# One body of an attention loop turned by one weight unit: each pass projects the next pass's queries among its own scores

## The reference

```python
def mixer_inputs(h, pos, p):
    q_r, k_r, v_r, g_r, q_d, k_d, v_d, ga, gb = jnp.split(h @ p['w_in'], points, axis=-1)
    q_d = rope(rmsnorm(q_d.reshape(B, L, N_DIFF_HEADS, 2, DIFF_HD), p['q_norm_g']), pos, DIFF_ROT, ROPE_THETA)
    k_d = rope(rmsnorm(k_d.reshape(B, L, N_DIFF_HEADS, 2, DIFF_HD), p['k_norm_g']), pos, DIFF_ROT, ROPE_THETA)
...
def layer_prompt(x, pos, p, lam_init):
    h = rmsnorm(x, p['norm1_g'])
    (q_r, k_r, v_r, g_r), (q_d, k_d, v_d), (ga, gb) = mixer_inputs(h, pos, p)
    o_r, S = retention_prompt(q_r, k_r, v_r)          # 4 heads, 128 wide keys, 256 wide values
    ...                                                # differential attention: 8 heads, two softmaxes each
    x = x + mixer_output(o_r, g_r, o_d, ga, gb, p, lam_init)
    f, conv_state = conv_glu(rmsnorm(x, p['norm2_g']), zeros, p)
    return x + f, (k_d, v_d, S, conv_state)
```

## Time and profile before

| | us |
|---|---|
| median of 3 runs | 2384.08 |
| the three runs | 2384.08, 2383.68, 2388.91 |
| profiled execution, whole | 2388.49 |
| its span, first to last instruction | 2386.6 |
| PE busy | 2297.6 |
| VectorE busy | 1131.4 |
| ACT busy | 966.5 |
| POOL busy | 851.3 |

### The profile page before, as it was taken

How to read it: one execution, slowest core, us unless ns; L and a number is a source line. 1 busy time by engine, 2 the same in 40 slices (tenths; PEclk the granted TensorE clock), 3 DMA queues, 4 the chain that set the end, 5 groups by cost and what they waited for, 6 DMA issues and landing times.

```text
span 2386.6 us, 50229 instructions
## 1 busy us (share of the span) xinstructions
PE 2297.6 (96%) x17560; PEld 2188.9 (92%) x17560; DVE 1131.4 (47%) x1918; ACT 966.5 (40%) x1829; POOL 851.3 (36%) x380
## 2 busy tenths in 40 slices
PE   5999999999999999999999999999999999999999
PEld 5788889889999999999988898798999999999999
DVE  3644453333545576156344644533345455742663
ACT  3544553333423343244335545533343234422443
POOL 3243232223433343343451342232333443434433
PEclk9999999999999999999999999999999999999999
DMA  4132212121222222322232122122122222223223
GB/s 150 51 102 70 85 60 68 60 90 60 89 72 89 83 88 70 108 89 73 80 99 72 63 83 85 51 83 86 60 72 75 72 89 89 84 75 101 90 67 105
DMA packets 81237, 193.28 MB, mean 81 GB/s; under 512 B 7232, under 2 KB 36000, under 8 KB 81056
## 3 DMA queue, kind: packets, MB, share of 16 engines
q1 hardware_dynamic: 59120, 172.38, 22.0%
q10 hardware_dynamic: 21936, 18.56, 2.4%
HBM read 177.50 MB, written 13.42 MB: 80 GB/s over the span
## 4 chain that ended last, share of the span: by engine, by line
issue 57%; PE 25%; POOL 14%; DVE 2%; ACT 1%; POOLq 0%; DVEq 0%; ACTq 0%
POOL wlo L490 11%; PE ps L602 6%; PE ps L604 6%; PE ps L603 6%; POOL rstd L496 3%; PE ps L961 2%; PE ps L962 2%; PE ps L963 2%; DVE ca L1943 1%; PE ps L641 0%; PE ps L642 0%; PE ps L643 0%; PE ps L669 0%; DVE af L1957 0%; DVE odif L1828 0%
## 5 line engine op out<-in xcount | busy, mean ns | idle before, releaser
L490 POOL TENSOR_TENSOR wlo<-raw,whi 128x1024 fp32r<-128x1024 f32 (+1 forms) x330 | 758.7, 2320 | 1338.4 <-ACT whi L1007 1338.4
L602 PE MATMUL ps<-hl,whi 128*128 128x272 f32 x2496 | 723.6, 290 | 2.4 <-DVE hl L1847 2.4
L604 PE MATMUL ps<-hl,wlo 128*128 128x272 f32 x2496 | 719.6, 288 | 0.0
L603 PE MATMUL ps<-hl,whi 128*128 128x272 f32 x2496 | 718.2, 288 | 0.0
L602 PEld LDWEIGHTS ps<-hl,whi 128*128 128x128 f32 x2496 | 471.6, 189 | 4.3 <-issue 2.8
L604 PEld LDWEIGHTS ps<-hl,wlo 128*128 128x128 f32 x2496 | 470.1, 188 | 0.0
L603 PEld LDWEIGHTS ps<-hl,whi 128*128 128x128 f32 x2496 | 469.7, 188 | 0.0
L641 PE MATMUL ps<-whi,hl 128*128 128x256 f32 x1536 | 446.6, 291 | 11.7 <-ACT rk L1234 10.2
L642 PE MATMUL ps<-wlo,hl 128*128 128x256 f32 x1536 | 438.9, 286 | 0.0
L643 PE MATMUL ps<-whi,hl 128*128 128x256 f32 x1536 | 438.1, 285 | 0.0
L1007 ACT ACTIVATE whi<-raw 128x1024 fp32r<-128x1024 f32 (+1 forms) x330 | 313.2, 996 | 224.0 <-PE ps L963 177.2
(11 more groups left out here) (214 smaller groups left out, 2926.5 us busy)
## 6 DMA issues: line engine op xcount, KB each, us to landing
raw<-in_w_units_dram SPq DMA_DIRECT2D x266, 512.0 KB, 4.7
raw<-in_w_down_units_dram SPq DMA_DIRECT2D x64, 352.0 KB, 3.3
out_new_k_prompt_dram<-rawk ACTq DMA_DIRECT2D x8, 512.0 KB, 3.0
out_new_v_prompt_dram<-vd ACTq DMA_DIRECT2D x8, 512.0 KB, 3.0
x<-in_x_dram ACTq DMA_DIRECT2D x8, 272.0 KB, 11.4
out_y_dram<-x SPq DMA_DIRECT2D x8, 272.0 KB, 5.7
kc_n<-in_cache_k_dram SPq DMA_DIRECT2D x8, 256.0 KB, 2.9
vc_n<-in_cache_v_dram SPq DMA_DIRECT2D x8, 256.0 KB, 3.3
```

The lines of the kernel that those rows point to most:

```text
L490: ins = e.tensor_tensor(wlo[:, s, a:b], raw[:, s, a:b], whi[:, s, a:b].bitcast(F32), ALU.subtract)
L602: e.matmul(out, wh, hi, start=(c == 0), stop=False)
L603: e.matmul(out, wh, lo, start=False, stop=False)
L604: ins = e.matmul(out, wl, hi, start=False, stop=(c == KC - 1))
```

## The change

- Phase S now has a unit, the queries of the first pass of D. They are computed chunk by chunk for four tiles at once, in the banks t, o, s0, s1 and s0b, and the statistics follow them. The last chunk's squares are added on VectorE, so PE's statistics need 6 matmuls in place of 12.
- A pass of D begins with the keys (unit 0), then values (1), gate (2), and the next pass's queries (3); in the last pass unit 3 is the queries and keys of retention head 0. Gate and queries are 72 chunks in one list, `FILL`: 16 ahead of the scores, five at each of the ten steps, the rest at the end.
- R is one body over four heads, without its first unit. The scaling of `oret` of a head is spread over the tiles of the next head's first unit.

```diff
-ORDER = [("S", 1), ("D", 4), ("R", 2), ("M", 1), ("F", 1), ("G", 1)]
+ORDER = [("S", 1), ("D", 4), ("R", 1), ("M", 1), ("F", 1), ("G", 1)]
...
+        UNITS = dict(S=1, D=4, R=11, M=16, F=FB + KC, G=FB + KC)
...
         def slot(phase, j):
-            return (j + (phase == "G")) % 2
+            return (j + (phase in ("D", "R", "G"))) % 2
...                                              PE, phase S
-                    stats("s0")
+                    e.wait_ge(*S.at("w_ready", k=0))
+                    for m in range(TILES):
+                        acquire(S_BANKS[m], act=1, dve=int(m == NT))
+                    for c in range(KC):
+                        for m in range(NT):
+                            if m in (0, 2):
+                                half_ready(c, m // 2)
...
+                    stats("s1b")
...                                              PE, phase D
-                    n_unit(0, hl1, xs, before=lambda m: e.wait_ge(*S.at("xs_ready", k=0)) if m == NT else None, chunk=half_ready)
+                    n_unit(0, hl1, xs)
...
-                    n_unit(1, hl1, xs)
-
...
-                    n_unit(2, hl1, xs, after=queries)
+                    n_unit(1, hl1, xs, after=queries)
                     cached_keys(0)
-                    e.wait_ge(*S.at("w_ready", k=3))
-                    t_tile(3, 0, 0, hl1, act=1)
+
+                    filled = [0, None]
...
+                    fill(FILL_FIRST)
...
-                        gate_chunks(GATE_SHARE[n])
+                        fill(FILL_SHARE[n])
...
+                    fill(len(FILL) - filled[0])
                     values(9)
...
-        GATE_SHARE = (3, 2, 2, 2, 1, 2, 2, 2, 4, 4)
+        FILL = ([("g", t, c) for t in range(4) for c in range(KC)] + [("q", t, c) for t in range(NT) for c in range(KC)]
+                + [("s", 0, c) for c in range(KC)])
+        FILL_FIRST = 16
+        FILL_SHARE = (5, 5, 5, 5, 5, 5, 5, 5, 5, 5)
...                                              ACT, phase D
+                    square(rawq, "q")
                     prev = None
                     t = 0
-                    for u, (name, buf) in enumerate((("q", rawq), ("k", rawk), ("v", vd))):
+                    for u, (name, buf) in enumerate((("k", rawk), ("v", vd))):
...
+                    hi("D", 3, 0)
+                    hi("D", 3, 1)
                     e.wait_ge(*S.at("t_ready", ("kc", 0)))
...
+                                if tt == 3:
+                                    hi("D", 4, 0)
+                                    hi("D", 4, 1)
...                                              ACT, phase R
+                                if u == 0 and m:
+                                    scale_ret(hh - 1, m - 1)
...
-                        e.wait_ge(*S.at("dve_step", ("rsr", hh)))
-                        for m in range(TILES):
...                                              VectorE, phase D
-                    sample_sum(rawq[0:DEC, NT, :], "mm0", ("N", 0, 4), "q")
                     qk_sums("q")
-                    qk_apply(rawq, "q", 0, lambda: sample_sum(rawk[0:DEC, NT, :], "mm1", ("N", 1, 4), "k"))
+                    qk_apply(rawq, "q", 0)
+                    sample_sum(rawk[0:DEC, NT, :], "mm0", ("N", 0, 4), "k")
                     qk_sums("k")
...
-                    sample_sum(vd[0:DEC, NT, :], "mm0", ("N", 2, 4), "v")
+                    sample_sum(vd[0:DEC, NT, :], "mm1", ("N", 1, 4), "v")
```

More of the change, by code:

```diff
@@ L375, in units @@
                     for c in range(KC)]
[L376 to L379 removed]
+            return [wide(FIRST[phase] + q) for q in range(UNITS[phase])]
         def prep_len(phase, j):
@@ L614, in stats @@
                 for m, a, b in blocks:
-                    for n, t in enumerate((acc[:, a:b], sq[:, 1, a:b])):
-                        ins = e.matmul(pv(bank, b - a, 1, m), t, one[:, :], start=(n == 0), stop=(n == 1))
+                    ins = e.matmul(pv(bank, b - a, 1, m), acc[:, a:b], one[:, :], start=True, stop=True)
                 ins.then_inc(*S.up("st_ready", "stats"))
@@ L775, in values @@
                         ins.then_inc(*S.up("o_ready", (hh, ib)))
[L777 to L795, removed]
                     scores(0)
@@ L986, in program, with filled_at @@
         SOFF = [0, 512, 896, 1152]
-        GATE_SHARE = (3, 2, 2, 2, 1, 2, 2, 2, 4, 4)
-        GATE_AT = [next(n for n in range(10) if sum(GATE_SHARE[:n + 1]) >= KC * t) for t in (1, 2, 3)]
+        FILL = ([("g", t, c) for t in range(4) for c in range(KC)] + [("q", t, c) for t in range(NT) for c in range(KC)]
+                + [("s", 0, c) for c in range(KC)])
+        FILL_FIRST = 16
+        FILL_SHARE = (5, 5, 5, 5, 5, 5, 5, 5, 5, 5)
+        FILL_DONE = {}
+        for end in range(KC, len(FILL) + 1, KC):
+            kind, t, _ = FILL[end - 1]
+            FILL_DONE[(kind, t)] = ([-1] if end <= FILL_FIRST else []) + [
+                n for n in range(10) if FILL_FIRST + sum(FILL_SHARE[:n + 1]) >= end] + [10]
+        def filled_at(n):
+            return [tile for tile, at in FILL_DONE.items() if at[0] == n]
         def act_program(S):
@@ L1549, in dve_program, with sample_sum @@
             with S.layers() as l:
+                def sample_sum(buf, bank, key, *name):
+                    e.wait_ge(*S.at(f"act_free_{bank}", ("rest",) + key))
+                    e.wait_ge(*S.own())
+                    e.scalar_tensor_tensor(out=buf, in0=pv(bank, DEC, UC), scalar=rs1[0:DEC, NT:TILES], in1=rest[:, 0:UC],
+                                           op0=ALU.mult, op1=ALU.add).then_inc(*S.up(f"dve_free_{bank}", ("rest",) + name))
                 with S.body("S"):
-                    norm_mean("s0")
+                    norm_mean("s1b")
                     e.wait_ge(*S.at("rs_ready", "rstd"))
                     e.tensor_scalar(hr[:, :], rs1[:, :], 0.5, None, ALU.mult).then_inc(*S.up("dve_step"))
+                    e.wait_ge(*S.at("pool_step", "zeroed"))
+                    sample_sum(rawq[0:DEC, NT, :], S_BANKS[NT], ("N", 0, NT), "q")
                 with S.body("D") as p:
@@ L1556, in dve_program @@
                     e.wait_ge(*S.at("pool_step", k=0))
-                    def sample_sum(buf, bank, key, name):
-                        e.wait_ge(*S.at(f"act_free_{bank}", ("rest",) + key))
-                        e.wait_ge(*S.own())
-                        e.scalar_tensor_tensor(out=buf, in0=pv(bank, DEC, UC), scalar=rs1[0:DEC, NT:TILES], in1=rest[:, 0:UC],
-                                               op0=ALU.mult, op1=ALU.add).then_inc(
-                            *S.up(f"dve_free_{bank}", ("rest", name)))
                     def qk_sums(name):
```

346 lines of the change are left out of this document (209 added, 137 removed).

## The result

| | us |
|---|---|
| changed kernel, median of 4 runs | 2577.91 (2574.07 to 2580.09) |
| kernel before, median of 4 runs | 2385.27 (2383.68 to 2388.91) |
| ratio, 95% interval | 1.0804 (1.0787 to 1.082) |
| profiled execution, whole and span | 2580.09, 2578.3 |

What follows compares the result with a forecast made beforehand. PE's own work plus its little waiting was taken to bound the kernel. 2386.6 + 189 (D) + 34 (clock) - 2 (layer starts) - 13 (R) = 2595 us of span; forecast time 2591 us, range of 8 in 10 2550 to 2635.

Steps and rivals of the forecast that it cites:

- The two chains: In D, the queries' and keys' paths over ACT, POOL and VectorE: two new PE waits, 27.0 us a pass together.
- the tiles and with the releasers named: PE waits at the values' second tile for the keys' sample sum, at the second gate tile for the values'.
- the steps of 13.8 and 13.2 us per pass: PE's predicted stands in each D pass: 13.8 us from the queries' chain, 13.2 us from the keys'.
- the sum: Forecast span of the whole program, all terms added to the earlier 2386.6 us: 2595 us.
- The scores: In D's softmax steps, thicker filling covers 1.2 of PE's 1.7 us idle a pass, bounds 0 and 1.7.
- The clock: Slow pace after D's stalls: 2.6 us for each of 16, +42 us; earlier falls go, -8; net +34.
- The starts of the layers: PE's statistics finish sooner, -3.6 and -5.5 us, but a wait for ACT gives back 3.4 each: -2.3 together.
- R: Retention phase: PE's 10.2 us of waits for ACT go, with their gaps and one clock fall: -12.7 us.
- the last rival: D's stalls as forecast, but the clock costs only 1.5 us for each: 2573 us; chance 12%.
- The one for the faster side: In D, the queries' rope is done ahead of use if their power isn't held behind `lo` 2: 2334 us; 5%.

Runs made afterwards that it cites:

- pow_q: Changed kernel with only the queries' power moved on POOL, from behind `lo` 2 to behind `lo` 1: 2520.58 us.
- pow_both: Changed kernel with both powers moved on POOL, the queries' ahead of `lo` 2 and the keys' ahead of `lo` 3: 2405.61 us.
- sums_first: Changed kernel with VectorE's sample sums of keys and values put ahead of the scaling and rope of queries and keys, POOL's order untouched: 2533.43 us.
- kept_busy_all: Changed kernel with 109 and 105 matmuls of unused result added on PE ahead of the two waits of each D pass: 2554.06 us.
- The mended kernels: The three kernels `turned_mended`, `turned_mended_fill` and `turned_final`, which keep the changed kernel's turned loop and reorder engine queues: 2409.34, 2400.42 and 2336.21 us.
- turned_final: `turned_mended_fill` with the values' sample sum between the keys' scaling and rope, and `lo` 3 started only after the keys' rope: 2336.21 us.
- turned_mended: Changed kernel with both powers earlier on POOL, the keys' sample sum ahead of the queries' rope, and ACT's rounding of units 1 and 2 reordered: 2409.34 us.
- turned_mended_fill: `turned_mended` with the five filling chunks of the first softmax step put ahead of the third scores instead of behind them: 2400.42 us.

## Why the prediction was right, and by how much it missed

*The two chains.* Both waits came eight times, at the tiles and with the releasers named. From the end of the keys' unit (E) to PE's next start the forecast had 16.7 us, the trace 186.06 - 169.93 = 16.1. The waits are 13.1 and 12.6 us where the steps of 13.8 and 13.2 us per pass stood; eight passes of 1.3 us are 11 of the 17 us by which the span (2578.3) is under the sum (2595). `pow_q` and `pow_both` show that it is POOL's order, and `sums_first` that it is not the banks.

*The scores.* Idle time fell by 1.0 us a pass, 1.2 were taken.

*The clock.* Taken at 2.6 us for each of 16 waits (the row gives 2.5), +42. The 24 matmuls behind the waits give 31.5 us in all, `kept_busy_all` gives 31: 2.0 for each wait. The term was mis-sized by 10 us. The 5.87 us from which it was read are only the projection's share of the program's start, and the fall inside the loop in the earlier trace rows, 3.41 us at 155.03, would have given 1.5 for each. The Trainium skill ("TensorE: Matmul & The Clock Gate", Part 1), as the prediction weighed it, says that the ramp penalty is below 1% of a typical kernel's span. This kernel's trace does not bear it out: 31 us are 1.2%. The prediction also counted the fall at 155.03 to the waits that recur so that every round starts slow. In the kernel before the clock fell behind only four of the eight rope waits; in the changed kernel it is down behind all 16.

*The starts of the layers.* The sum of -2.3 us fits, and by luck. The keys' unit of layer 0 begins at 42.44 instead of the 45.4 forecast, because the slow pace ended after 3.1 us of work and not after 10.2. That of layer 1 begins 18.9 us after the last phase's last matmul instead of 15.5, behind a wait of 2.5 us at its first matmul and one fall of the clock; a second fall follows at 1326.6, 1.5 us that the forecast did not have. The added wait for ACT was 3.1 us each time, 3.4 forecast.

*R.* Forecast -12.7. From R's first matmul to the next phase before: 214.1 and 215.6 us, of which 13.4 each are the unit that moved into D; after: 194.9 twice. That is 5.8 and 7.3 less, together -13.1.

*The number.* The waits were 11 us too long in the forecast and the clock 10; the scores (2 us) and the fall at 1326.6 went the other way, and some 2 us stay open. Both large errors have the same sign, and 2578 lies nearer to the last rival, the one with 1.5 us a wait for the clock (2573), than to the forecast (2591). That is luck: with the waits as measured, that rival would have said about 2562.

*The rivals.* The one for the faster side said that the rope would be ahead of its use if the power were not held behind `lo` 2, and put that at 2334 us. The mended kernels show the mechanism was right but the condition too small: with the two powers moved the time was 2406. To reach 2336 it also took keeping both ropes away from a `lo`, two sample sums moved ahead of the ropes, and the filling among the scores (9 us). That the result is so near to 2334 is luck too.

## What to carry to other kernels

When a unit of work is moved to another pass, go through every engine's program for what was ordered by the old distance: here a power of 3.5 us stood behind a `lo` whose slot is freed by the very unit that lost its lead. A stage with a long chain over three engines wants its links ahead of the bulk work in each queue, and bulk work on POOL kept off the moments when VectorE's short steps decide. Don't judge what the clock costs by its mean over the run, which counts the idle time too: what counts is how much work falls in the slow stretches. And read the passes of a loop one by one before a difference of two whole runs is divided among them: one stop of 4 us and two long falls of the clock in layer 0 of `kept_busy_all` hid a quarter of what was looked for.

## What the hardware showed that was not expected

- A wait of 1.8 to 2.4 us lost two thirds as much time to the slow pace as one of 13: 21 us over 16 waits against 31.5 (second pass: 4.45 and 4.64 us against 4.71 and 5.22, with 2.97 and 3.10 at full pace). The mean clock of the run rose from 0.955 to 0.986 and the time fell by 4 us.
- At the program's start the slow pace lasted 10.2 us in the one trace where PE began with the statistics matmuls. In the ten traces where it began with the projection it lasted 3.1 (changed kernel) to 5.9 us (`turned_final`), so 3.1 is no fixed figure, and one trace does not show that the kind of matmul made the difference.
- VectorE's rope steps of 160 columns take 0.33 us, and 2.34 to 2.45 us beside POOL's subtraction. In every meeting two of the six steps were hit, in the kernel before as in `pow_q`, `pow_both`, `turned_mended` and `turned_mended_fill`; in `turned_mended` each ends within 0.2 us of the end of a half of `lo`. The means ahead of the power are hit the same way: in the changed kernel `ms` takes 1.76 us at 161.69, beside `lo` 1, and 0.18 us at 189.25, beside nothing.
